# Two layer norms of a fused two-block transformer: the affine step of three block pairs on ScalarE instead of VectorE, and a weight's low half one pair later

## The reference

```python
def layer_norm(x, g, b):
    mu = xf.mean(-1, keepdims=True)
    var = jnp.square(xf - mu).mean(-1, keepdims=True)
    return (xf - mu) * lax.rsqrt(var + EPS) * g + b

# first block
h = hybrid_mixer(x, w_in, ...)                      # mLSTM heads and sliding-window heads, then @ w_out
x = layer_norm(ALPHA * x + h, ln1_g, ln1_b)         # the first norm
h = memory_cross_attention(x, mem, xa_wq, xa_wkv, xa_wo)
x = layer_norm(ALPHA * x + h, ln2_g, ln2_b)         # the second norm
h = conv_ffn(x, ffn_w_up, ..., ffn_w_down)
x = layer_norm(ALPHA * x + h, ln3_g, ln3_b)
# second block: three mixers side by side, w_o, RMS norms, gated FFN
x = hybrid_layer(x, c, mod_w, ..., w_o, w_ffn_in, w_ffn_out)
```

## Time and profile before

| | |
|---|---|
| median of 3 runs | 918.74 us |
| profiled execution, its own time | 919.39 us |
| its span on the core | 917.5 us |
| mean granted TensorE clock | 0.965 |
| TensorE, VectorE, ScalarE busy | 94%, 72%, 54% |
| first norm, last statistics to pair (6,7) done | about 197 to 214 us of the span |
| second norm | about 273 to 290 us |

### The profile page before, as it was taken

How to read it: one execution, slowest core, us unless ns; L and a number is a source line. 1 busy time by engine, 2 the same in 40 slices (tenths; PEclk the granted TensorE clock), 3 DMA queues, 4 the chain that set the end, 5 groups by cost and what they waited for, 6 DMA issues and landing times.

```text
span 917.5 us, 16415 instructions
## 1 busy us (share of the span) xinstructions
PE 861.1 (94%) x6648; PEld 825.5 (90%) x6648; DVE 657.1 (72%) x1021; ACT 498.8 (54%) x710; POOL 6.2 (1%) x15
## 2 busy tenths in 40 slices
PE   4999997999899999999997899999999999999995
PEld 4889986889798999999997899898898899999995
DVE  4775677678567888887867896787797866655443
ACT  5544446444444666655446756777657644444451
POOL 0200000000000000000000000000000000000000
PEclk9999999989998999999998999999999799999998
DMA  9774565756152665666762386475565377765531
GB/s 324 210 234 134 169 200 175 229 169 210 44 176 78 207 185 184 184 199 224 270 204 69 116 252 197 126 221 171 161 216 174 102 252 231 235 215 166 180 115 47
DMA packets 145580, 166.42 MB, mean 181 GB/s; under 512 B 5488, under 2 KB 135536, under 8 KB 145504
## 3 DMA queue, kind: packets, MB, share of 16 engines
q1 hardware_dynamic: 143888, 162.82, 56.7%
q0 software_dynamic: 544, 1.49, 0.8%
q10 hardware_dynamic: 1072, 1.05, 0.3%
HBM read 164.10 MB, written 1.25 MB: 180 GB/s over the span
## 4 chain that ended last, share of the span: by engine, by line
PE 41%; ACT 6%; DVE 6%; issue 1%; DVEq 0%; ACTq 0%
PE ps L168 28%; PE ps L423 13%; DVE lor L147 2%; ACT FA L144 2%; ACT hir L144 2%; DVE FA L147 1%; ACT L144 1%; DVE FA L155 1%; ACT X L144 0%; DVE X L147 0%; ACT HIH L144 0%; DVE FA L151 0%; DVE FA L158 0%; DVE SQ L161 0%; ACT SQ L144 0%
## 5 line engine op out<-in xcount | busy, mean ns | idle before, releaser
L147 DVE TENSOR_TENSOR lor<-raw,hir 128x1024 fp32r<-128x1024 f32 (+1 forms) x268 | 309.9, 1174 | 117.0 <-ACT hir L144 100.9
L144 ACT ACTIVATE hir<-raw 128x1024 fp32r<-128x1024 f32 (+1 forms) x268 | 266.3, 1015 | 126.7 <-PE ps L423 117.4
L168 PE MATMUL ps<-INH,hir 128*128 128x256 f32 (+1 forms) x1064 | 308.3, 290 | 16.5 <-DVE lor L147 13.0
L423 PE MATMUL ps<-INL,hir 128*128 128x256 f32 (+1 forms) x1064 | 304.6, 286 | 2.8 <-DVE INL L147 2.5
L168 PE MATMUL ps<-INH,lor 128*128 128x256 f32 (+1 forms) x1064 | 303.2, 285 | 0.0
L168 PE MATMUL ps<-HIH,hir 128*128 128x256 f32 x864 | 249.6, 289 | 6.6 <-DVE lor L147 4.3
L168 PE MATMUL ps<-HIH,lor 128*128 128x256 f32 x864 | 245.8, 284 | 0.0
L423 PE MATMUL ps<-HIL,hir 128*128 128x256 f32 x864 | 245.7, 284 | 0.0
L168 PEld LDWEIGHTS ps<-INH,hir 128*128 128x128 f32 x1064 | 206.2, 194 | 20.5 <-issue 10.3
L423 PEld LDWEIGHTS ps<-INL,hir 128*128 128x128 f32 x1064 | 205.4, 193 | 4.0 <-DVE INL L147 4.0
L168 PEld LDWEIGHTS ps<-INH,lor 128*128 128x128 f32 x1064 | 206.1, 194 | 1.0 <-issue 1.0
(11 more groups left out here) (161 smaller groups left out, 669.6 us busy)
## 6 DMA issues: line engine op xcount, KB each, us to landing
raw<-in_w_in SPq DMA_DIRECT2D x64, 512.0 KB, 4.6
raw<-in_mod_wT SPq DMA_DIRECT2D x48, 512.0 KB, 4.4
raw<-in_ffn_w_up SPq DMA_DIRECT2D x44, 512.0 KB, 4.5
raw<-in_w_ffn_in SPq DMA_DIRECT2D x44, 512.0 KB, 4.6
raw<-in_ffn_w_down SPq DMA_DIRECT2D x20, 512.0 KB, 5.1
raw<-in_w_ffn_out SPq DMA_DIRECT2D x20, 512.0 KB, 3.5
raw<-in_xa_wkv SPq DMA_DIRECT2D x16, 512.0 KB, 4.1
raw<-in_xa_wq SPq DMA_DIRECT2D x8, 512.0 KB, 5.0
```

Of the source, the lines that this page charges most:

```text
L144: return AC.do(lambda e: e.activation(o, i, f, **kw), *w)
L147: return DV.do(lambda e: e.tensor_tensor(o, a, b, op), *w)
L168: return PE.do(lambda e: e.matmul(o, l, r, start=start, stop=stop, skip_group_check=True), *w, inc=inc)
L423: return PE.do(lambda e: e.matmul(o, *b, start=False, stop=stop, skip_group_check=True), inc=stop)
```

## The change

In `layer_norm`, ScalarE applies gain and bias in place for the three pairs, in two instructions right behind the pair's two high halves; VectorE keeps this step for blocks 0 and 1. The deferred low half of the weight is issued behind the tail of pair (2,3) instead of the tail of block 1.

```diff
--- before.py
+++ after.py
@@ -1007,11 +1007,12 @@
             bm, (br, t_r), low = finish(True, LN_EPS, t)
             pend = None
 
-            def tail(u, a, h):
+            def tail(u, a, h, x):
                 k, n = u
                 d = X[:, k:k + n, :]
                 for i in range(n):
-                    x = ts(d[:, i, :], d[:, i, :], V(gn, k + i), V(bn, k + i), ALU.mult, ALU.add, a, t_vec, h)
+                    if n == 1:
+                        x = ts(d[:, i, :], d[:, i, :], V(gn, k + i), V(bn, k + i), ALU.mult, ALU.add, a, t_vec, h)
                 x = tt(inp.lo[:, k:k + n, :], d, inp.hi[:, k:k + n, :].bitcast(F32), ALU.subtract, x, h, *inp.free)
                 for i in range(n):
                     inp.tok[k + i] = (h, x)
@@ -1024,11 +1025,15 @@
                 br.free = [t]
                 for i in range(n):
                     h = act(inp.hi[:, k + i, :], d[:, i, :], ACT.Identity, t, t_vec, *inp.free, scale=V(gn, k + i), bias=V(bn, k + i))
+                x = None
+                if n == 2:
+                    for i in range(n):
+                        x = act(d[:, i, :], d[:, i, :], ACT.Identity, h, scale=V(gn, k + i), bias=V(bn, k + i))
                 if pend:
                     tail(*pend)
-                    if k == 2 and low:
+                    if k == 4 and low:
                         low()
-                pend = ((k, n), t, h)
+                pend = ((k, n), t, h, x)
             tail(*pend)
 
         for c in range(4):
```

## The result

| | before | after |
|---|---|---|
| median | 917.84 us (15 runs, 916.03 to 920.41) | 914.71 us (15 runs, 912.3 to 918.32) |
| ratio, 95% interval | | 0.9966, 0.9952 to 0.998 |
| profiled execution, span | 919.39, 917.5 us | 912.94, 911.1 us |

The change is faster by 3.1 us, 1.8 to 4.4 by the interval. The kernel before, which stood at 918.74 in three runs, stands at 917.84 in fifteen.

A forecast was written before the change was run, and what follows sets the result against it. The prediction took TensorE's queue plus its pauses to bound the kernel. Gains of 0.85 us in the first norm and 1.14 in the second sum to 1.99; 918.74 less this gives 916.75, say 916.7 us, range 915.0 to 918.5.

The forecast's parts named there:

- The mechanism: First two norms: VectorE's busy queue delays pair (2,3)'s low half, and TensorE waits 0.59 and 0.88 us at block 2.
- the 2.26 and 0.69 us of the earlier trace: Untouched third norm: 2.26 us from first high half to start of VectorE's low half, 0.69 more to its end.
- no pause took the old one's place: Rival: TensorE then stands at pair (4,5)'s low half or a weight; half given back, 917.7 us; chance 0.12.
- the end of the 120 us: Behind the second norm, TensorE runs 120 us without a pause, so nothing there could take the gain.
- The rival on ScalarE's length: In each norm, ScalarE's 1.09 us against VectorE's 0.73 ends last; 0.36 us longer a norm, 919.5 us; chance 0.05.
- the later slot: Rival: the load waiting for the weight's raw slot goes 2.2 us later and delays TensorE; 921.2 us; chance 0.05.
- the pauses of this execution: First two norms: removing the block 2 pauses gains 0.85 and 1.14 us, 1.99 us in sum.
- the 3.1 us for an early rise: Upper bound for both norms: TensorE's clock rising 1.5 us earlier makes the gain 3.1 us in all.
- the clock does not mostly add: First two norms: the prediction said the clock's rise mostly adds to the gain of 1.99 us.
- the 2.0 that the prediction set as the least over many runs: Both norms: with the clock's rise varying, the gain lies between 2.0 and 3.1 us over many runs.
- the base: Whole kernel: the median before, 918.74 us, from which the gain of 1.99 us was taken.
- The 0.6 us of scatter in the low end: Range's low end: 918.74 less 3.1 and 0.6 us of scatter gives 915.0 us.

The follow-up runs named there:

- busy TensorE: 23 idle products a norm added in TensorE's pauses around the first two norms' statistics: kernel before 919.01 us, ratio 1.0004; changed kernel 914.41 us, ratio 0.9955.
- slipped products: Idle products added in the FFN behind the second norm: changed kernel with ten 916.85 us, with five 916.52 us; kernel before with ten 918.68 us.
- the old form with ten idle products: Kernel before with 10 idle products added in the FFN behind the second norm: 918.68 us, ratio 1.0012.

## Why the prediction missed

**The mechanism** of the wait was right. VectorE's queue, with the deferred weight and the next pair ahead, made pair (2,3) late; ScalarE's in-place pass took the 2.26 and 0.69 us of the earlier trace rows; every start of VectorE and ScalarE in the new order came within 0.05 us; no pause took the old one's place at block 4, at block 6 or at a weight; the gain went through to the end of the 120 us. Both halves of the change behaved as the order said: ScalarE's part carries it, the later low half alone brings next to nothing, and only together do they clear block 2 and block 4. The rival on ScalarE's length fell, since its longer pass ran beside VectorE's next pair. It is not without effect: VectorE's low half of (2,3) waits 0.19 us for it, which TensorE feels only when the clock rises early. The Trainium skill (ScalarE: Activation LUTs, Rules for kernel authors) sends multiply and add to VectorE; the lengths agree with it (1.09 us a pair against 0.73), the times don't (0.9978 for ScalarE's part alone). No cost of the later slot shows.

**The term that was misread is the pause**, "I take 1.99, the pauses of this execution". A pause is not a fixed cost. The old stage always took 15.2 us from the restart, with rises at 4.3, 5.3, 5.9, 6.0, 6.2 us or with the clock up throughout, because VectorE set its end: the third product of block 2 starts 6.9 us behind the restart in each of these traces, and a clock that rises earlier only makes TensorE wait longer for it. The new one takes 11.71 us and 0.445 of the time to the rise, but not under 13.8. The gain per norm is the difference of the two: 0.54 us (rise at 6.7) to 1.4 us. With the rises of the first trace, 6.0 and 5.3, the rule gives 0.85 and 1.14, the forecast's own figures: they were right for the execution that they were read from, and that it lies near the mean is luck. The mean over the five traces with the full change and no busy TensorE is 28.53 us for both stages, 1.9 us less than 30.44. The bounds were off: the 3.1 us for an early rise was a little too high, since a floor of 13.8 gives 2.8 at most, and the clock does not mostly add. A later rise takes away, and in the first trace after, with 5.8 and 6.7, the two stages gave 1.5 us, under the 2.0 that the prediction set as the least over many runs.

The mean granted clock on record for every execution fits this beyond the traces. In the old form (107 executions) 0.001 more of it goes with 0.48 us less (95% interval 0.42 to 0.55), in the changed kernel (39) with 0.86 us less (0.73 to 0.99). By estimate, 0.001 of 915 us is 0.92 us of TensorE's work at full clock; in the new form nearly that much shows in the time, in the old form half of it.

**The step that failed, as far as the runs show it, is the base.** The prediction took 1.99 off 918.74, a median of 3 runs; 15 gave 917.84. That is 0.9 of the 2.0 us by which 916.7 was missed. The 0.6 us of scatter in the low end was read from the same three runs, which spread over 1.5 us where the fifteen after spread over 6. From 917.84 the same working gives 915.85 and a low end of 914.1, and 914.71 would have lain inside. The other 1.1 us lie in the gain, which measured 3.1 us against 1.99.

**The rest, 1.1 us in the first comparison, is open.** Three comparisons gave 0.34%, 0.28% and 0.34%, 2.6 to 3.1 us, and each interval holds 1.9 us, in the first and the third near its edge. In the traces two places could hold more. Products 3250 to 4000 took 103.06 us in all four traces with the full change and no slipped products, and 103.4 to 107.2 in five with VectorE's affine steps in both norms (the kernel before three times, with the later low half, and with busy TensorE); with ScalarE's part alone and with the first norm alone it was 107.2 too. Of such a difference the next 600 products give back up to 1.5 us (84.6 us behind 103.06, 83.1 behind 107.2). And product 60 came at 20.1 to 21.1 us in the six traces with the full change, and at 20.5 to 21.9 in the six with VectorE's affine steps in both norms, where the program is the same. The slipped kernels show that the first place can swing by 4 us, and their medians don't show that the change moves its mean. Against more falls of the clock in the old form as the whole cause stands the mean granted clock, 0.9664 over its 107 executions and 0.9661 over the 39 of the changed kernel; at one and the same clock, 0.967, they took 918.0 us (23 executions) and 914.4 (14) on the mean. For the start of the program, what was expected of three traces came true (20.7, 20.4 and 21.8 us), but the old form with ten idle products had it at 20.5, no kernel was made to test it, and why a change 180 us later should move it is not known.

## What to carry to other kernels

Look for what sets the end of a stage before pricing a pause in it. Where another engine does, the pause takes up whatever TensorE's clock gives, so its length in one trace is its worth only for a clock that rises as it did there; work out both forms from the restart and compare the ends. A step that is 50% longer on an idle engine is still the faster one, if it leaves a queue that the consumer waits for; and an item that is moved back in that queue only moves the wait unless something also leaves the queue. Take the base of an absolute forecast from as many runs as its range needs.

## What the runs showed of the hardware

- TensorE's granted clock rose 4.3 to 6.7 us behind the restart of the same code (windows at 0.50 of 4.2 us in one execution, 6.7 in another). The Trainium skill (TensorE: Matmul & The Clock Gate, Part 1) says that the instant varies from run to run; the traces agree. With 23 idle products of 128x256 in the norm's pauses it was 1.00 throughout the stage in both kernels. Keeping TensorE busy paid nothing in the old form (1.0004) and at most a little in the new.
- The same 750 products took from 103.06 to 107.67 us in different executions, at a mean granted clock from 0.97 to 0.92, with falls of the clock in some executions where others had none.
- TensorE's products of 128x256 in the stages started 0.213 us apart at a granted clock of 0.50 and 0.118 at 1.00, so half the clock stretched their spacing 1.8 times, not twice.
- ScalarE's in-place `Identity` with gain and bias from SBUF took 594 ns a block of 128x256 (12 of them), and at 1.0 to 1.1 us a pair it did not slow VectorE's subtractions, which took 0.68 to 0.69 us beside it as before.
